# Turning six rows of modulation sums per layer in the down projection, behind units 8 to 13

## The chip, the cores and the metric

The kernel runs on one core of a Trainium2 chip. The metric is the device time of one execution in microseconds (us). The core has four computing engines that work side by side, each through its own instructions in order, and that wait for one another on semaphores: TensorE (PE in the profile; its weight loads are shown apart as PEld), VectorE (DVE), ScalarE (ACT) and GpSimd (POOL). SyncE (SP) issues the weight loads.

## What is computed

Two transformer blocks one after the other on 256 tokens of width 1024, all in float32. The first has two layers with a mixer and a feed-forward part each; the second is one layer whose norms are scaled and shifted by a modulation that hangs on a vector `c` alone:

```python
for l in range(DEPTH):                       # DEPTH = 2
    mixed = hybrid_mixer(x, mem, ...)
    x = layer_norm(ALPHA * x + mixed, ln1_g[l], ln1_b[l])
    ff = jnp.square(jax.nn.relu(x @ w_up[l])) @ w_down[l]      # 1024 -> 4096 -> 1024
    x = layer_norm(ALPHA * x + ff, ln2_g[l], ln2_b[l])
...
mod = (jax.nn.silu(c) @ ada_w + ada_b)[:, None, :]             # 1024 -> 6 * 1024, second block
```

## The kernel before

**Feed-forward units.** Each layer's feed-forward part runs in 16 units, u = 0 to 15 (`FFN_UNITS`): units 0 to 7 are the up projection, 8 to 15 the down projection (`UP_UNITS` = 8). A unit is one weight block of 1024 x 512. PE makes seven products of it instead of eight (`seven`, by sums and differences of quarter blocks); DVE makes the sums of the weight's quarters that this needs, four instructions in `weight_sums(u)` (L1335), one unit ahead: in its step u it calls `weight_sums(u + 1)`. For an up unit DVE then puts the seven products together (`combine`); for down units it does so in the last two steps only, since the others add up in the accumulators.

**Modulation.** The matrix `ada_w_2` is loaded beside, in twelve blocks of 1024 x 512, six per layer, j = 0 to 5, at the positions `ADA_POSITIONS` = 1, 3, 5, 8, 10, 12 among the units. ACT scales the eight slices of a block by silu(c) (`ada_scale`, L890). DVE adds the eight slices up to one row of 512 per partition (`ada_sums(j)`, L1277, three instructions, in step u = `ADA_POSITIONS[j]`) and writes it to one of two buffers, `ada_rows`, which lie in the tile `pre`. PE turns the row by four 128 x 128 transposes into the bank `ptb` (`ada_turned(j)`, L2630), and DVE reduces the bank to four columns of `mod` (`ada_columns(j)`, L1287). There is one such bank, so PE waits on `ada_back` before it turns row j until DVE has reduced row j - 1:

```python
pe.wait_ge(ada_summed, len(ADA_AT) * l + j + 1)
if l or j:
    pe.wait_ge(ada_back, len(ADA_AT) * l + j)
```

PE turns row j behind unit `ADA_POSITIONS[j]` + 1, that is behind units 2, 4, 6, 9, 11 and 13; DVE reduces it in step `ADA_POSITIONS[j]` + 2, that is 3, 5, 7, 10, 12 and 14.

**DVE's order in step u** (L1559): `ada_sums` if u is one of the positions, `weight_sums(u + 1)`, `ada_columns` if it is due, in layer 1 `bias_steps` in steps 9, 11 and 13, and `combine` where there is one.

**Weight loads.** All weights come through `ring`, three slots of 2 MB, in the order of use, modulation blocks among them; SP issues each load when its slot is free (`slot_free`, L459). The slot of a unit is freed by PE: the first product of the next unit carries the increment of `used` (`to_release` in `mm`, L2190; the transposes of a turning do not carry it). The slot of a modulation block is freed by DVE's last sum. In the down projection, the load for unit u + 2 goes into the slot of unit u, as in 8 and 10 or 10 and 12.

**POOL** makes the token-side sums of the down projection, one group of four for each pair of units; the later groups wait for the end of an odd unit.

Of the kernel before, what the change touches and what calls it, by code (L numbers as in the profile page):

```python
# [14 lines left out]
ALU = mybir.AluOpType  # L15
# [5 lines left out]
P = 128  # L21
# [14 lines left out]
UCOLS = 512  # L36
# [7 lines left out]
UP_UNITS, DOWN_UNITS = FF // UCOLS, 2 * (FF // (UROWS * P))  # L44
# [42 lines left out]
FFN_AT, ADA_AT = ffn_positions()  # L87
# [7 lines left out]
ADA_POSITIONS = [*ADA_UP, *(UP_UNITS + j for j in ADA_DOWN)]  # L95
# [104 lines left out]
def build(nc, a, out, stop=None):  # L200
    with ExitStack() as ctx:
# [8 lines left out]
        ident = sb("ident", [P, P])  # L210
# [9 lines left out]
        st = sb("st", [P, 2, T])  # L220
# [42 lines left out]
        kiz = sb("kiz", [P, 2, T])  # L263
        widx = sb("widx", [P, TT, 16])
        pre = sb("pre", [P, 2, 2, T + TAPS2 - 1])
# [27 lines left out]
        otok = hid[:, 16:24, :].rearrange("p a b -> p (a b)").rearrange("p (t d) -> p t d", t=TT)  # L293
        mod = sb("mod", [P, DEPTH, 24])
        silc = sb("silc", [P, 2, DC])
        ada_rows = pre[:, :, :, :].rearrange("p a b c -> p (a b c)")[:, 0:2 * UCOLS].rearrange("p (i n) -> p i n", i=2)
        nm = sb("nm", [P, 2, 2])
        zz = sb("zz", [P, 2, 2])
        rz = sb("rz", [P, 2, 2])
# [22 lines left out]
        ptb = ctx.enter_context(nc.psum_tensor("ptb", [P, 4, P], F32))  # L322
# [74 lines left out]
        ada_summed, ada_full, ada_back = sem("ada_summed"), sem("ada_full"), sem("ada_back")  # L397
# [830 lines left out]
        def _(dve):  # L1228
            steps = Steps(dve, dve_seq)
            tt, ts, stt = dve.tensor_tensor, dve.tensor_scalar, dve.scalar_tensor_tensor  # L1230
# [5 lines left out]
            for m in range(2):  # L1236
                dve.wait_ge(pe_begun, m + 1)
                j = 2 * m + 1
# [7 lines left out]
            for t in range(TT):  # L1246
                ins = dve.bn_aggr(mv[:, t, :], bn[:, t, :, :].rearrange("p a b -> p (a b)"))
# [29 lines left out]
            def ada_sums(j):  # L1277

                n = ADA_AT[j]
                dve.wait_ge(loaded[n % RING], 16 * (LAYER_UNITS // RING * l + n // RING + 1))  # L1280
                w = ring[:, n % RING]
                dve.wait_ge(ada_scaled, DC * (len(ADA_AT) * l + j + 1))
                for width in (4, 2):
                    steps.link(tt(w[:, 0:width, :], w[:, 0:width, :], w[:, width:2 * width, :], ALU.add))  # L1284
                tt(ada_rows[:, j % 2, :], w[:, 0, :], w[:, 1, :], ALU.add).then_inc(ada_summed, 1)

            def ada_columns(j):  # L1287

                dve.wait_ge(ada_full, len(ADA_AT) * l + j + 1)
                dve.tensor_reduce(mod[:, l, 4 * j:4 * j + 4], ptb[:, :, :], X, ALU.add).then_inc(ada_back, 1)  # L1290
# [177 lines left out]
            for l in range(DEPTH):  # L1468
# [90 lines left out]
                for u in range(FFN_UNITS):  # L1559
                    if u in ADA_POSITIONS:  # L1560
                        ada_sums(ADA_POSITIONS.index(u))
                    if u + 1 < FFN_UNITS:
                        weight_sums(u + 1)
                    if u - 2 in ADA_POSITIONS:
                        ada_columns(ADA_POSITIONS.index(u - 2))
                    if l == DEPTH - 1 and u in (9, 11, 13):
                        bias_steps((u - 9) // 2)
                    if u < UP_UNITS:
                        combine(u)
                    elif u >= FFN_UNITS - 2:  # L1570
                        h = u - (FFN_UNITS - 2)
                        if h == 0:
                            dve.wait_ge(xaff_ready, 4 * (l + 1))
                            combine(UP_UNITS, lambda: with_x(0, 0, pair01))
                        else:
                            def top_half():
                                with_x(0, 1, pair01)
                                token_mean2(0)
                            combine(UP_UNITS + 1, top_half)
                        dve.wait_ge(mz_free, GROUPS * l + UP_UNITS + h + 2)  # L1580
                        with_x(1, h, pair45)
                        if h == 0:
                            for t in range(TT):
                                dve.wait_ge(y_ready, 4 * l + 1 + t)
                                steps.mark(dve.bn_stats(bn[:, t, 0, :], ytok[:, t, 0, :]))
                            if l == DEPTH - 1:
                                bias_steps(3)
                                bias_steps(4)
# [261 lines left out]
            for u in range(2):  # L1850
                k, c = u - 2, 4 * u
# [257 lines left out]
            for t in range(TT):  # L2109
                for h in range(2):  # L2110
                    n = 2 * t + h
# [15 lines left out]
                for j in range(2, 4):  # L2127
                    dve.wait_ge(turn_full, 4 + (4 + 1 if t else j + 1))
                    for i in range(2):
                        c = 2 * j + i  # L2130
# [54 lines left out]
        def _(pe):  # L2185
# [43 lines left out]
            for j in range(4):  # L2229
                b = scr[j // 2] if j % 2 else head_bank()  # L2230
                for i in range(2):
                    for t in range(TT):
                        c = 2 * j + i
                        ins = pe.transpose(b[:, i, t * P:(t + 1) * P], mtok[:, t, c * P:(c + 1) * P], ident[:, :])
# [32 lines left out]
            b = head_bank()  # L2267
            for i in range(2):
                ins = pe.transpose(b[:, i, 0:127], prow[0:127, i, :], ident[0:127, 0:127])
            ins.then_inc(filled, 1)  # L2270
            for i, n in ((2, 123), (3, 128), (4, 33)):
                b = head_bank()
# [3 lines left out]
            for j in range(4):  # L2276
                b = head_bank()
                for i in range(2):
                    for t in range(TT):
                        c = 2 * j + i  # L2280
                        ins = pe.transpose(b[:, i, t * P:(t + 1) * P], xtok[:, t, c * P:(c + 1) * P], ident[:, :])
# [139 lines left out]
            for l in range(DEPTH):  # L2421
# [63 lines left out]
                else:  # L2485
                    w = next_unit()
# [4 lines left out]
                    b = free_bank()  # L2491
# [60 lines left out]
                for k in range(STEPS + 2):  # L2552
# [13 lines left out]
                    if k in (4, 6, 8, 10):  # L2566
                        h = (k - 4) // 2
                        b = free_bank()
# [10 lines left out]
                    elif k == 3:  # L2579
# [3 lines left out]
                        b = free_bank()  # L2583
                        for c in range(2):
                            ins = pe.matmul(b[:, 0, :], ones[:, 1, :], cy[:, c, :], start=c == 0, stop=c == 1)
# [7 lines left out]
                    elif k == 6:  # L2593
                        pe.wait_ge(csq_ready, l + 1)
                        b = free_bank()
                        for c in range(2):
                            ins = pe.matmul(b[:, 0, :], ones[:, 1, :], csq[:, c, :], start=c == 0, stop=c == 1)
# [32 lines left out]
                def ada_turned(j):  # L2630

                    pe.wait_ge(ada_summed, len(ADA_AT) * l + j + 1)
                    if l or j:
                        pe.wait_ge(ada_back, len(ADA_AT) * l + j)
                    for c in range(4):
                        ins = pe.transpose(ptb[:, c, :], ada_rows[:, j % 2, c * P:(c + 1) * P], ident[:, :])  # L2636
                    ins.then_inc(ada_full, 1)

                for u in range(FFN_UNITS):
                    assert units_done[0] == FFN_AT[u]  # L2640
                    w = next_unit()
                    t, t_base = tsum[u % 2], 4 * (FFN_UNITS * l + u)
                    if u < UP_UNITS:
                        for order in (("m1", "m2"), ("m4", "m5", "m7", "m6", "m3")) if u == 0 else (usual,):
                            seven(w, t, t_base, GROUPS * l + u, 1 - u % 2, pv_z[:, 0, :], True, True,
                                  x[:, 0:4, 0:H], x[:, 4:8, 0:H], x[:, 4:8, H:T], [sx[:, i] for i in range(4)],
                                  sx_ready, 4 * l, order, True, True,
                                  ((xlow_ready, DC * l), (xhigh_ready, DC * l)) if u == 0 else (None, None),
                                  a22_written=(xhigh_ready, DC * l + 4) if u == 0 else None)
                            if u == 0 and "m1" in order:  # L2650
                                features_back(1, 1)
                                features_back(1, 0)
                    else:
                        q, h = (u - UP_UNITS) // 2, (u - UP_UNITS) % 2
                        c, first, last = 8 * q, q == 0, q == 3
                        seven(w, t, t_base, GROUPS * l + UP_UNITS + h, 1 - h, pv_z[:, h, :], first and h == 0, last if h else first,
                              hid[:, c:c + 4, 0:H], hid[:, c + 4:c + 8, 0:H], hid[:, c + 4:c + 8, H:T],
                              [sh[:, q % 2, 0], sh[:, q % 2, 1], hid[:, c:c + 4, H:T], sh[:, q % 2, 2]],
                              sh_ready, 16 * l + 4 * q, usual, first, last, tokens=True)
                    to_release[0] += 1  # L2660
                    if u - 1 in ADA_POSITIONS:
                        ada_turned(ADA_POSITIONS.index(u - 1))
                    if u in ADA_POSITIONS:
                        assert units_done[0] == ADA_AT[ADA_POSITIONS.index(u)]
                        units_done[0] += 1
# [65 lines left out]
            for n, c in enumerate((4, 5, 0, 1)):  # L2731
                pe.wait_ge(xsq_sum, n // 2 + 1)
                ins = mm(ms, ones[:, 0, :], ysq[:, c, :], n == 0, n == 3)
# [4 lines left out]
            w = next_unit()  # L2738
            features(w, [0, 1], y, (h2_ready, 0))
            b = free_bank()  # L2740
            for k in range(DC):
                mm(b[:, 0, :], w[:, k, 256:384], y[:, k, :], k == 0, k == DC - 1)
            for k in range(DC):
                ins = mm(b[0:112, 1, :], w[:, k, 384:496], y[:, k, :], k == 0, k == DC - 1)
# [5 lines left out]
            b = mean_squares(None, 0, 1, latsq[0], 2, which=1, last=False)  # L2750
# [9 lines left out]
            b = free_bank()  # L2760
            for t in range(TT):
                pe.transpose(b[:, 0, t * P:(t + 1) * P], kvn[:, t * P:(t + 1) * P], ident[:, :])
            for t in range(TT):
                ins = mm(b[:, 1, 48 * t:48 * t + 48], kvki[64:112, 1, t * P:(t + 1) * P], ident[64:112, 64:112], True, True)
            ins.then_inc(filled, 1)
            b = free_bank()
# [371 lines left out]
```

## Time and profile before

| | us |
|---|---|
| median of 3 runs (lowest to highest) | 1309.13 (1308.36 to 1311.02) |
| the profiled execution | 1308.58 |
| its span | 1306.6 |
| PE busy in the span | 1293.0 |
| DVE busy | 941.5 |
| ACT busy | 426.4 |
| POOL busy | 185.2 |

The profile is one execution seen by the hardware's profiler. Its page gives busy times, the chain of work that ended last (followed back from the last instruction to what released it) and the costliest groups of instructions. The rows in order of time show for each engine the start, the length, the line of the kernel, what is written from what, and in brackets how long the engine idled before and what ended that. Rows of like instructions are merged, with their count. PE's matmuls overlap their weight loads, so the pauses of PE are best read from the starts of the weight loads (PEld).

### The profile page before, as it was taken

The page shows a single profiled execution, that of the slowest core. Times are in us where ns is not written, and L with a number is a line of the kernel's source. Part 1 is how long each engine was busy: PE and PEld are TensorE (multiplying, and loading weights), DVE is VectorE, ACT ScalarE, POOL GpSimd, SP SyncE. Part 2 cuts the span into 40 slices and gives each one's busy share as a digit, 9 for nine tenths or more (in the row PEclk, how much of TensorE's full clock was granted, in tenths as well). Part 3 has the DMA queues.
Part 4 walks back from the last instruction along what each step waited for, and adds up shares of the span by engine and source line. Part 5 has one row for each costly group of instructions (what it writes and reads, how often), then busy time and mean ns, then how long its engine had stood idle before and what let it go on. Part 6 is the DMA issues. An engine that isn't in the chain of part 4 may idle for free.

```text
span 1306.6 us, 32615 instructions
## 1 busy us (share of the span) xinstructions
PE 1293.0 (99%) x14429; PEld 1153.6 (88%) x14429; DVE 941.5 (72%) x1602; ACT 426.4 (33%) x929; POOL 185.2 (14%) x164
## 2 busy tenths in 40 slices
PE   8999999999999999999999999999999999999998
PEld 7975899988898589998877899999999986999986
DVE  3985798556688479857881799788888845866753
ACT  2254334220226433332055424455742103100101
POOL 3100422030000042204134000003200100011100
PEclk9999999999999999999999999999999999999999
DMA  9632567576433257767638895137645554645540
GB/s 326 202 130 97 194 239 278 206 267 238 163 129 129 97 195 260 260 223 268 216 98 241 220 248 150 60 121 253 208 134 186 175 192 130 194 151 176 179 178 32
DMA packets 132923, 243.06 MB, mean 186 GB/s; under 512 B 7237, under 2 KB 37725, under 8 KB 132273
## 3 DMA queue, kind: packets, MB, share of 16 engines
q1 hardware_dynamic: 122506, 218.00, 48.7%
q0 software_dynamic: 9872, 22.80, 7.4%
q8 instruction: 114, 1.87, 0.6%
q14 instruction: 24, 0.20, 0.1%
q10 hardware_dynamic: 407, 0.20, 0.1%
HBM read 231.49 MB, written 6.34 MB: 182 GB/s over the span
## 4 chain that ended last, share of the span: by engine, by line
PE 91%; DVE 5%; DMA 1%; ACT 1%; POOL 1%; issue 1%; SPq 0%; DVEq 0%
PE acc L2192 56%; PE scr L2192 17%; PE pvw L2192 9%; DVE mid L1512 2%; PE ptb L2306 1%; PE scr L2804 1%; PE pvw L2811 1%; DMA ring<-in_w_mem_kv 1%; PE scr L2297 1%; PE ptb L2192 1%; PE pvw L2316 1%; PE ptb L2636 0%; DMA strip_rows<-hid 0%; DVE hid L1860 0%; PE pvw L2322 0%
## 5 line engine op out<-in xcount | busy, mean ns | idle before, releaser
L2192 PE MATMUL acc<-y,ring 128*64 128x128 f32 (+3 forms) x1760 | 154.5, 285 | 0.0
L2192 PEld LDWEIGHTS acc<-y,ring 128*64 128x64 f32 (+2 forms) x1760 | 141.8, 152 | 7.7 <-ACT y L959 1.2
L2192 PE MATMUL acc<-ring,big 128*128 128x256 f32 (+1 forms) x376 | 115.6, 453 | 0.0
L2192 PEld LDWEIGHTS acc<-ring,big 128*128 128x128 f32 x376 | 70.6, 190 | 33.4 <-issue 27.0
L2192 PE MATMUL acc<-ring,hid 128*128 128x256 f32 (+1 forms) x364 | 99.1, 417 | 0.0
L2192 PE MATMUL acc<-x,ring 128*64 128x128 f32 (+1 forms) x1472 | 98.9, 278 | 0.0
L2192 PEld LDWEIGHTS acc<-x,ring 128*64 128x64 f32 (+1 forms) x1472 | 89.6, 139 | 4.7 <-issue 3.2
L895 ACT ACTIVATE ring<-ring,silc 128x512 f32<-128x512 f32 x96 | 60.1, 709 | 95.2 <-DMA ring<-in_ada_w 95.1
L2192 PEld LDWEIGHTS acc<-ring,hid 128*128 128x128 f32 x364 | 68.4, 190 | 22.2 <-issue 14.9
L2192 PE MATMUL acc<-ysq,ring 128*64 128x128 f32 x1248 | 75.0, 273 | 0.1
L2192 PEld LDWEIGHTS acc<-ysq,ring 128*64 128x64 f32 x1248 | 69.8, 137 | 0.4 <-ACT ysq L1076 0.4
L1284 DVE TENSOR_TENSOR ring<-ring 128x2048 f32<-128x2048 f32 (+1 forms) x24 | 44.1, 1836 | 33.5 <-ACT ring L895 32.9
L2192 PE MATMUL scr<-ysq,ring 128*64 128x128 f32 x1056 | 63.8, 273 | 0.0
L2192 PEld LDWEIGHTS scr<-ysq,ring 128*64 128x64 f32 x1056 | 59.3, 137 | 0.0
L1512 DVE SCALAR_TENSOR_TENSOR mid<-upad,pc,mid 128x256 f32<-128x256 f32 x120 | 48.7, 477 | 0.0
L1135 ACT ACTIVATE big<-acc 128x512 f32<-128x512 f32 x19 | 11.3, 596 | 109.7 <-PE acc L2192 109.7
L1344 DVE TENSOR_TENSOR ring<-ring 128x1024 f32<-128x1024 f32 x32 | 46.5, 1454 | 0.0
L1343 DVE TENSOR_TENSOR mid<-ring 128x1024 f32<-128x1024 f32 x16 | 19.5, 1222 | 37.1 <-DMA ring<-in_w_down 24.6
L720 ACT ACTIVATE work<-work,nm 128x256 f32<-128x256 f32 x80 | 39.6, 497 | 19.3 <-DVE nm L1258 15.6
L575 POOL TENSOR_TENSOR big<-hid 128x512 f32<-128x512 f32 x8 | 15.4, 1931 | 209.0 <-PE pvw L2192 147.9
L2192 PE MATMUL acc<-mid,ring 128*128 128x128 f32 (+2 forms) x384 | 42.4, 283 | 0.0
L2192 PEld LDWEIGHTS acc<-mid,ring 128*128 128x128 f32 (+1 forms) x384 | 39.6, 178 | 1.3
(581 smaller groups left out, 2767.5 us busy)
## 6 DMA issues: line engine op xcount, KB each, us to landing
ring<-in_w_in SPq DMA_DIRECT2D x24, 2048.0 KB, 11.4
ring<-in_w_up SPq DMA_DIRECT2D x16, 2048.0 KB, 8.5
ring<-in_w_down SPq DMA_DIRECT2D x16, 2048.0 KB, 8.0
ring<-in_ada_w SPq DMA_DIRECT2D x12, 2048.0 KB, 13.4
ring<-in_w_ffn_in SPq DMA_DIRECT2D x22, 1024.0 KB, 6.9
ring<-in_w_out SPq DMA_DIRECT2D x6, 2048.0 KB, 8.2
ring<-in_w_o_ssd SPq DMA_DIRECT2D x4, 2048.0 KB, 9.1
ring<-in_w_ffn_out SPq DMA_DIRECT2D x4, 2048.0 KB, 7.8
```

Of the source, the lines that this page charges most:

```text
L575: pool.tensor_tensor(s1, a21, a22, ALU.add).then_inc(sh_ready, 1)
L720: ins = act.activation(pr[:, i % 2, j, :], lg[:, i % 2, j, :], ACT.Exp, scale=-1.0, bias=nm[:, i % 2, j:j + 1], accum_out=zz[:, i % 2, j:j ...
L895: act.activation(ring[:, n % RING, k, :], ring[:, n % RING, k, :], ACT.Copy, scale=silc[:, 1, k:k + 1]).then_inc(ada_scaled, 1)
L1284: steps.link(tt(w[:, 0:width, :], w[:, 0:width, :], w[:, width:2 * width, :], ALU.add))
L1343: tt(t[:, 0], b12, b11, ALU.subtract).then_inc(t_ready, 1)
L1344: tt(b12, b22, b12, ALU.subtract).then_inc(t_ready, 1)
L1512: ins = stt(cy[:, c, :], upad[:, c, tap:tap + T], w, cy[:, c, :], ALU.mult, ALU.add)
L2192: ins = pe.matmul(dst, w, m, start=start, stop=stop, is_transpose=turned, skip_group_check=True)
L2297: ins = pe.matmul(scr[m][:, t, :], q[half, t * P:(t + 1) * P], keys[half, h, :], start=True, stop=True)
L2306: ins = pe.transpose(ptb[:, 2 * j + kt, :], at[:, i % 2, j, kt * P:(kt + 1) * P], ident[:, :])
L2316: ins = pe.matmul(pvb[:, 0, :], vt[:, h * P:(h + 1) * P], pt[:, i % 2, kt, :], start=kt == 0, stop=kt == TT - 1)
L2804: ins = pe.matmul(scr[i % 2][:, m, :], q2[:, 2 * j + m, t * P:(t + 1) * P], kvn[:, :], start=True, stop=True)
```

## The change

The rows go to four buffers instead of two; the two new ones lie in the tiles `kiz` and `st`. All six turnings of a layer stand behind down units: row j is turned behind unit 8 + j, units 8 to 13, and DVE reduces it in step 9 + j, steps 9 to 14, still behind `weight_sums`. The waits in `ada_turned` and in `ada_columns` stay as they are. The sums of the rows stay in their steps.

```diff
-        ada_rows = pre[:, :, :, :].rearrange("p a b c -> p (a b c)")[:, 0:2 * UCOLS].rearrange("p (i n) -> p i n", i=2)
+        pre_flat = pre[:, :, :, :].rearrange("p a b c -> p (a b c)")
+        ada_rows = [pre_flat[:, 0:UCOLS], pre_flat[:, UCOLS:2 * UCOLS], kiz[:, :, :].rearrange("p a t -> p (a t)"),
+                    st[:, :, :].rearrange("p a t -> p (a t)")]
...
-                tt(ada_rows[:, j % 2, :], w[:, 0, :], w[:, 1, :], ALU.add).then_inc(ada_summed, 1)
+                tt(ada_rows[j % 4], w[:, 0, :], w[:, 1, :], ALU.add).then_inc(ada_summed, 1)
...
                     if u + 1 < FFN_UNITS:
                         weight_sums(u + 1)
-                    if u - 2 in ADA_POSITIONS:
-                        ada_columns(ADA_POSITIONS.index(u - 2))
+                    if 0 <= u - 1 - UP_UNITS < len(ADA_AT):
+                        ada_columns(u - 1 - UP_UNITS)
...
                     for c in range(4):
-                        ins = pe.transpose(ptb[:, c, :], ada_rows[:, j % 2, c * P:(c + 1) * P], ident[:, :])
+                        ins = pe.transpose(ptb[:, c, :], ada_rows[j % 4][:, c * P:(c + 1) * P], ident[:, :])
                     ins.then_inc(ada_full, 1)
...
                     to_release[0] += 1
-                    if u - 1 in ADA_POSITIONS:
-                        ada_turned(ADA_POSITIONS.index(u - 1))
+                    if 0 <= u - UP_UNITS < len(ADA_AT):
+                        ada_turned(u - UP_UNITS)
```


## Rows read from the trace of the kernel before

**Rows 1.** the page: PE busy; the chain that ended last, by engine

```profile
PE 1293.0 (99%) x14429; PEld 1153.6 (88%) x14429; DVE 941.5 (72%) x1602; ACT 426.4 (33%) x929; POOL 185.2 (14%) x164
...
PE 91%; DVE 5%; DMA 1%; ACT 1%; POOL 1%; issue 1%; SPq 0%; DVEq 0%
```

**Rows 2.** PEld by time, layer 0, up projection: start, length, work, [gap before]

```profile
173.44 1.81 PEld L2192 LDWEIGHTS scr<-ysq,ring 128*64 128x64 f32 x32
...
175.19 1.81 PEld L2192 LDWEIGHTS pvw<-x,mid 128*64 128x64 f32 x32
...
177.17 0.42 PEld L2636 LDWEIGHTS ptb<-ident,pre 128*128 128x128 f32 x4 [0.17 <-issue]
...
177.75 1.73 PEld L2192 LDWEIGHTS acc<-x,ring 128*64 128x64 f32 x32 [0.17 <-issue]
```

**Rows 3.** the same view, down projection of layer 0, starts of units and turnings

```profile
252.49 1.70 PEld L2192 LDWEIGHTS acc<-ring,hid 128*128 128x128 f32 x8
...
262.85 1.70 PEld L2192 LDWEIGHTS pvw<-work,hid 128*128 128x128 f32 x8
...
264.58 0.57 PEld L2636 LDWEIGHTS ptb<-ident,pre 128*128 128x128 f32 x4
...
265.12 1.60 PEld L2192 LDWEIGHTS acc<-ring,hid 128*128 128x128 f32 x8
...
277.10 1.70 PEld L2192 LDWEIGHTS acc<-ring,hid 128*128 128x128 f32 x8
...
301.72 1.70 PEld L2192 LDWEIGHTS acc<-ring,hid 128*128 128x128 f32 x8
...
314.35 1.60 PEld L2192 LDWEIGHTS acc<-ring,hid 128*128 128x128 f32 x8
```

**Rows 4.** DVE in order of time, down projection of layer 0, same columns

```profile
261.31 1.23 DVE L1343 TENSOR_TENSOR mid<-ring 128x1024 f32<-128x1024 f32 x1 [4.05 <-DMA ring<-in_w_down]
...
271.78 3.55 DVE L1284 TENSOR_TENSOR ring<-ring 128x2048 f32<-128x2048 f32 x2 [5.71 <-ACT ring L895]
...
275.98 1.22 DVE L1343 TENSOR_TENSOR work<-ring 128x1024 f32<-128x1024 f32 x1
...
280.64 0.68 DVE L1290 TENSOR_REDUCE mod<-ptb 128x4 f32<-128x512 f32 x1
...
310.65 1.23 DVE L1343 TENSOR_TENSOR mid<-ring 128x1024 f32<-128x1024 f32 x1 [4.79 <-DMA ring<-in_w_down]
```

**Rows 5.** SP's queue in order of time: two merged issues of weight loads

```profile
265.86 12.45 SPq L475 DMA_DIRECT2D ring<-in_w_down  x2
```

**Rows 6.** us to landing: issued at 265.86, at 254, all of 240 to 330

```profile
ring<-in_w_down SPq DMA_DIRECT2D x1, 2048.0 KB, 7.8
...
ring<-in_ada_w SPq DMA_DIRECT2D x1, 2048.0 KB, 12.9
...
DMA to landing us min/median/max: 7.8/8.0/13.0
```

**Rows 7.** DVE in order of time, down projection of layer 1

```profile
596.80 4.50 DVE L1284 TENSOR_TENSOR ring<-ring 128x2048 f32<-128x2048 f32 x2 [2.44 <-ACT ring L895]
...
606.61 0.68 DVE L1290 TENSOR_REDUCE mod<-ptb 128x4 f32<-128x512 f32 x1
```

**Rows 8.** POOL in order of time, down projection of layer 1

```profile
596.80 3.42 POOL L580 TENSOR_TENSOR big<-hid,big 128x512 f32<-128x512 f32 x1
```

**Rows 9.** PE's weight loads in order of time, layer 1: units 9 and 11

```profile
577.43 1.70 PEld L2192 LDWEIGHTS acc<-ring,hid 128*128 128x128 f32 x8
...
602.04 1.70 PEld L2192 LDWEIGHTS acc<-ring,hid 128*128 128x128 f32 x8
```

**Rows 10.** busy time by stretch: engines' us (instructions), granted clock, DMA share, GB/s

```profile
0.00:1300.00 1300.00, 1292.75 (x14429) 1153.64 (x14429) 937.56 (x1595) 424.99 (x923) 185.21 (x164) 1.00 0.57 186
...
1300.00:1306.60 6.60, 0.23 (x2) 0.00 (x0) 3.93 (x8) 1.43 (x6) 0.00 (x0) 0.70 0.43 159
```

**Rows 11.** PE's waits: for whom, total us, times, longest

```profile
PE pvw L2226 <- DVE upad L1234: 1.8, 1, 1.8
```


## The prediction

> **What bounds the kernel now.** The page comes first: PE is busy in 99% of the span, and the chain of work that ended last lies 91% on PE [rows 1]. So a change counts if it makes PE's row of products shorter or opens a hole in it. Next I read PE's weight loads in order of time, because they show where PE pauses. In the up projection one product follows the other every 1.75 us (173.44 to 175.19), but where a turning of a modulation row stands between two units the pitch is 2.56 (175.19 to 177.75) [rows 2]: the turning costs 0.81, of which two gaps of 0.17 stand before and behind its four transposes. In the down projection the pitch is 1.727 ((262.85 - 252.49) / 6), and with a turning 2.27 (262.85 to 265.12): 0.54, without such gaps [rows 3]. The up projection works in tiles 64 columns wide and the transposes in tiles of 128, as the down projection does; that is the one visible difference. Last I read what DVE does in the down projection, because the change makes PE wait for a DVE instruction there [rows 4].
>
> **The change part by part.**
>
> **1. Twelve turnings, all behind down units.** Six (three in each of two layers) move from a place of 0.81 to one of 0.54: 6 x 0.27 = 1.6 us saved, if nothing else moves. The transposes and their loads are the same 4 each. No DMA is issued in them.
>
> **2. Three reductions per layer leave the up projection on DVE** (0.68 us each). PE covers them: its products follow one another there with no other gap than those at the turnings [rows 2], so I take cost and gain as nothing. Had PE been late for DVE there, it would be a gain of at most 6 x 0.68 = 4 us; that is the lower bound. PE arrives 0.81 earlier after each turning removed; the weight loads are released by PE and shift with it, so DVE shifts too. Two more buffers: the sums are written as before, at the same length.
>
> **3. The wait.** This decides. Turning j on PE waits for `ada_back` of j - 1, because both use the one bank `ptb`: PE may not overwrite it until DVE has reduced row j - 1 into `mod`. Before, a unit or more lay between a turning and the next, and the reduction was long done. Now turning j stands behind unit 8 + j, the reduction of j - 1 in DVE's step u = 8 + j, **behind** `weight_sums(9 + j)` and, for j = 2 and 4, behind `ada_sums` too. DVE works in order, so PE, which has no need yet of these weight sums, now waits for them at the end of the unit. What is queued behind PE's wait is everything: the next unit's products, and its first product frees the ring slot of the unit just done, so the next weight load on SP's queue waits too. POOL's and ACT's work is released by the same events, relative to the unit, as before.
>
> How late is DVE? I count from the start S of PE's first product in the unit.
>
> *Odd turnings (1, 3, 5).* Unit 9 starts at 252.49 and PE gets to its end at 264.58, 12.09 later [rows 3]. The first product of unit 9 frees the slot for the load of unit 10: issue comes 0.74 after the start (265.12 [rows 3] to 265.86 [rows 5]) and landing 7.8 after the issue [rows 6]. So DVE starts `weight_sums(10)` at 261.31, 8.82 after S, after 4.05 us of idling for that load [rows 4]. The four sums take 4.66 up to the next instruction (275.98 to 280.64 [rows 4]). The reduction that now stands behind them would start at 13.48 and end, 0.68 later, at 14.16. PE is there at 12.09. It waits 2.1, plus the semaphore's way, which I set at 0.1 (bounds 0 and 0.2, the order of the 0.17 gaps in [rows 2]).
>
> *Even turnings (2, 4).* Here DVE has first to sum the modulation weights, whose load is issued behind that of unit 10 and takes 12.9 to land [rows 6]; ACT scales them, and DVE idles for ACT until 271.78 [rows 4]. None of this hangs on when unit 10 starts, only on S of unit 9. The reduction that follows today starts at 280.64, 28.15 after 252.49 [rows 3, 4]. In the new order one stands at the same place: end 28.15 + 0.68 = 28.83, with the semaphore 28.93, and the turning of 0.54 makes unit 11 start at **29.47** after unit 9's start. Before: 277.10 - 252.49 = **24.61** [rows 3]. So a pair of units gets **4.86 us** longer. The odd wait inside the pair isn't added: what PE loses at turning 1 it would else lose at turning 2. Only the load for unit 11 could follow it: it is issued when unit 10 starts, 14.80 + 0.74, lands 7.8 later at 23.34, and DVE wants it at 23.49 (275.98 - 252.49). It fits, by 0.15; a load half a us longer would add 0.35 per pair.
>
> *Layer 1.* The same chain, a little longer: the first two sums of the modulation weights take 4.50 there [rows 7] instead of 3.55 [rows 4], beside a POOL sum of 3.42 that starts with them [rows 8], and the reduction starts at 606.61 [rows 7], 29.18 after unit 9's start at 577.43 [rows 9]. 29.18 + 0.68 + 0.1 + 0.54 = 30.50 against 602.04 - 577.43 = 24.61 [rows 9]: **5.89 us** per pair. POOL's work is released by the end of unit 9, so I leave the collision in.
>
> *The last, turning 5,* stands behind unit 13 and waits for the reduction in step 13: unit 13 starts at 301.72, DVE gets its load at 310.65, 8.93 later [rows 3, 4]; + 4.66 + 0.68 + 0.1 + 0.54 = 14.91 to the start of unit 14, against 314.35 - 301.72 = 12.63 [rows 3]: **2.28 us**. Layer 1 shows the same pattern, so twice.
>
> **The sum.** Two pairs per layer: 2 x 4.86 + 2 x 5.89 = 21.5. Two last ones: 4.6. These hold the turnings 1 to 5 on both sides. Outside them: six turnings of 0.81 gone from the up projection (-4.9), turning 0 behind unit 8 new (2 x 0.54 = +1.1). Net 21.5 + 4.6 - 4.9 + 1.1 = **+22.3 us**. The profiled execution took 1308.58 (span 1306.6), 0.04% below the median of 1309.13, so I use it as it is: 1308.6 + 22.3 = **1330.9 us**. Bounds of this case: without the collision on POOL in layer 1 2 x 1.03 less, a DVE gain in the up projection 4 less; slower loads in four pairs 1.4 more, semaphore 0.2 instead of 0.1 another 0.6, and 2 for what the stages behind make of it: some 1325 to 1335.
>
> **The rivals.**
>
> *No wait, only the gain.* If each reduction were done when PE comes, 1308.6 - 1.6 = **1307.0**. It decides at 12.09 us after the unit's start: load and weight sums and reduction together would have to fit, which now take 8.82 + 4.66 + 0.68 = 14.16; the load would have to land in 5.6 instead of 7.8. Against it speaks that no load of this stretch landed in less than 7.8 [rows 6]. For it, only that I could have misread which step the reduction stands in. 5%.
>
> *The clock falls in the holes.* The granted clock is 1.00 from 0 to 1300 us, and 0.70 in the last 6.6 us, where PE does two instructions [rows 10]: so the lower level (1.2 GHz) exists and comes when PE stops. The longest wait of PE in the trace is 1.8 us [rows 11]; the new ones are 2 to 3. The Trainium skill ("TensorE: Matmul & The Clock Gate", section on HAM oscillation) tells of a matmul loop that waits for a load in each step and starts every step at the lower clock; by that rule this change would pay at each hole once more. The price from rows: a product of 1.73 at half the clock takes 1.73 more; one such behind each of ten waits makes +17, **1348**. Nothing in this trace shows a fall in a hole inside the work, and PE was busy for twelve us before each. 7%.
>
> *The change does less than it says:* part of the waits is met, since sums or loads run faster when PE leaves more time between units, some 10 us in all: **1319**. The load rows speak against it. 5%.
>
> **How the numbers follow.** My forecast holds 83%, the three rivals 5, 7 and 5%. About 0.2% (2.6 us) is what a measurement here can tell from no change: the first rival lies within it, all else is slower. Faster 2%, same 5%, slower 93%. The range starts from 1325 to 1335, with some 4 at either end for what the bounds don't know: 1321 to 1339. That leaves out the first two rivals, part of the third, and a few per cent of the forecast: some 18%.
>
> **What would show it.** Right: idle time of PE before the turning's line, put down to DVE's write of `mod`, ten times (turnings 1 to 5 in two layers) with some 2 us at each; unit 9 to unit 11 some 29.5 us apart in layer 0 and 30.5 in layer 1; up units with no turning between them and no gap; the granted clock at 1.00 throughout. Wrong: units in the down projection still 12.1 us apart with turnings between them (then the reduction isn't behind the weight sums), or products longer than 1.73 behind the holes (then the clock).

## The result and the profile after

The changed kernel takes 1332.63 us (median of 4 runs, 1330.51 to 1335.57) against 1309.16 before: a ratio of 1.018, 95% interval 1.0168 to 1.0192. It is 23.5 us slower. The profiled execution took 1333.1, its span is 1331.1, 24.5 more than the span before.

Four lines of the page after, to be read beside [rows 1]: PE's busy time and share, the granted clock in 40 slices, and the chain that ended last, by engine and by line. A slice is 33 us long, so a fall of the clock for a few us does not show in that row.

```profile
PE 1298.3 (98%) x14429; PEld 1156.5 (87%) x14429; DVE 938.6 (71%) x1602; ACT 426.2 (32%) x929; POOL 181.2 (14%) x164
...
PEclk9999999999999999999999999999999999999999
...
PE 78%; DVE 10%; DMA 7%; ACT 2%; issue 2%; POOL 1%; SPq 0%; DVEq 0%
PE acc L2194 49%; PE scr L2194 14%; PE pvw L2194 7%; DMA ring<-in_ada_w 4%; DVE mid L1514 2%; ACT ring L897 1%; DVE ring L1286 1%; DMA ring<-in_w_down 1%; PE ptb L2308 1%; PE pvw L2813 1%; PE scr L2806 1%; DMA ring<-in_w_mem_kv 1%; DVE ring L1346 1%; PE scr L2299 1%; PE ptb L2194 1%
```

PE does the same 14429 instructions, and its share of the chain falls from 91 to 78%. What has come in is DVE, ACT and a load: `ring<-in_ada_w`, the load of the modulation block, now has 4% of the span. Work that ran beside PE has got onto the path. The list of PE's waits (for whom: us in total, times, longest) says at which point:

```profile
PE ptb L2638 <- DVE mod L1292: 18.6, 10, 3.2
```

Ten waits of the turning for DVE's write of `mod`, as many as there are turnings 1 to 5 in two layers. Such a row does not exist in the kernel before, whose longest wait is the one in [rows 11]. In order of time, PE's weight loads in the down projection of layer 0 (start, length, work, gap before), to be read beside [rows 3]:

```profile
250.50 0.57 PEld L2638 LDWEIGHTS ptb<-ident,pre 128*128 128x128 f32 x4
251.04 1.60 PEld L2194 LDWEIGHTS acc<-ring,hid 128*128 128x128 f32 x8
...
265.24 0.42 PEld L2638 LDWEIGHTS ptb<-ident,pre 128*128 128x128 f32 x4 [2.25 <-issue]
265.63 1.60 PEld L2194 LDWEIGHTS acc<-ring,hid 128*128 128x128 f32 x8
...
279.92 0.42 PEld L2638 LDWEIGHTS ptb<-ident,kiz 128*128 128x128 f32 x4 [2.33 <-issue]
280.31 1.60 PEld L2194 LDWEIGHTS acc<-ring,hid 128*128 128x128 f32 x8
...
294.75 0.42 PEld L2638 LDWEIGHTS ptb<-ident,st 128*128 128x128 f32 x4 [2.48 <-issue]
295.13 2.48 PEld L2194 LDWEIGHTS acc<-ring,hid 128*128 128x128 f32 x8
297.70 2.44 PEld L2194 LDWEIGHTS acc<-ring,big 128*128 128x128 f32 x8
300.17 1.70 PEld L2194 LDWEIGHTS acc<-ring,hid 128*128 128x128 f32 x8
...
309.40 0.42 PEld L2638 LDWEIGHTS ptb<-ident,pre 128*128 128x128 f32 x4 [0.63 <-issue]
309.79 1.60 PEld L2194 LDWEIGHTS acc<-ring,hid 128*128 128x128 f32 x8
...
324.38 1.60 PEld L2194 LDWEIGHTS acc<-ring,hid 128*128 128x128 f32 x8
```

In these rows a line with `ptb<-ident` is a turning, and the one behind it is the first product of the next unit. Turning 0 (250.50) has no gap. Turning 1 stands behind a gap of 2.25, turning 2 behind 2.33. Unit 9 starts at 251.04, unit 11 at 280.31, 29.27 later; before it was 24.61. DVE in the same stretch, to be read beside [rows 4]:

```profile
259.77 1.23 DVE L1345 TENSOR_TENSOR mid<-ring 128x1024 f32<-128x1024 f32 x1 [4.51 <-DMA ring<-in_w_down]
...
264.44 0.68 DVE L1292 TENSOR_REDUCE mod<-ptb 128x4 f32<-128x512 f32 x1
...
279.12 0.68 DVE L1292 TENSOR_REDUCE mod<-ptb 128x4 f32<-128x512 f32 x1
```

The reduction at 264.44 stands at the end of the four weight sums that waited 4.51 us for a load, and PE turns the next row 0.8 us after that start (265.24). The chain that ended last, in order of time, runs through the other one, at 279.12: from the load of the modulation block over ACT's scaling and DVE's sums (start, us, what):

```profile
252.19 12.94 DMA ring<-in_ada_w
...
265.15 5.02 ACT ring L897 x8
...
270.26 2.30 DVE ring L1286
...
279.12 0.69 DVE mod L1292
```

In the up projection, the pitch from the last product of a unit to the first of the next is 1.74 now, where it was 2.56 [rows 2]:

```profile
199.86 1.81 PEld L2194 LDWEIGHTS pvw<-x,mid 128*64 128x64 f32 x32
201.60 1.81 PEld L2194 LDWEIGHTS acc<-x,ring 128*64 128x64 f32 x32
```

### The profile page after: what moved, and what is told of

It is laid out like the page before. It is cut to its first block, busy times and chain, and to the rows that moved or that the text cites. A ratio compares the mean times of both kernels' runs of the same rounds, so it can differ in the third digit from the quotient of the medians.

```text
span 1331.1 us, 32615 instructions
## 1 busy us (share of the span) xinstructions
PE 1298.3 (98%) x14429; PEld 1156.5 (87%) x14429; DVE 938.6 (71%) x1602; ACT 426.2 (32%) x929; POOL 181.2 (14%) x164
## 4 chain that ended last, share of the span: by engine, by line
PE 78%; DVE 10%; DMA 7%; ACT 2%; issue 2%; POOL 1%; SPq 0%; DVEq 0%
PE acc L2194 49%; PE scr L2194 14%; PE pvw L2194 7%; DMA ring<-in_ada_w 4%; DVE mid L1514 2%; ACT ring L897 1%; DVE ring L1286 1%; DMA ring<-in_w_down 1%; PE ptb L2308 1%; PE pvw L2813 1%; PE scr L2806 1%; DMA ring<-in_w_mem_kv 1%; DVE ring L1346 1%; PE scr L2299 1%; PE ptb L2194 1%
## 5 line engine op out<-in xcount | busy, mean ns | idle before, releaser
L2194 PE MATMUL acc<-ring,hid 128*128 128x256 f32 (+1 forms) x364 | 102.5, 429 | 0.0
L881 ACT ACTIVATE pt<-acc 128x512 f32<-128x512 f32 x20 | 11.7, 586 | 97.0 <-PE acc L2194 97.0
```

Of the source, the lines that this page charges most:

```text
L2194: ins = pe.matmul(dst, w, m, start=start, stop=stop, is_transpose=turned, skip_group_check=True)
```

## The experiments

**Where the reduction stands in DVE's order.** The changed kernel, with DVE's step in another order:

```diff
+                    if 0 <= u - 1 - UP_UNITS < len(ADA_AT):
+                        ada_columns(u - 1 - UP_UNITS)
                     if u in ADA_POSITIONS:
                         ada_sums(ADA_POSITIONS.index(u))
                     if u + 1 < FFN_UNITS:
                         weight_sums(u + 1)
-                    if 0 <= u - 1 - UP_UNITS < len(ADA_AT):
-                        ada_columns(u - 1 - UP_UNITS)
```

> The changed kernel (1332.6 us) with one thing moved: in each step DVE reduces the row that is due before it makes the sums of the modulation block and of the next weight, not behind them. Turnings, buffers and waits are those of the changed kernel. Theory (the reduction's place in DVE's order makes PE wait): no wait of PE on the write of mod is left, and the six turnings that moved out of the up projection are won: 1309.2 - 1.7 = 1307.5. Rival (six turnings in a row, or slots freed behind turnings, slow the down projection): it stays within some us of 1332. Rival (the clock that falls in holes is most of the loss): 1307.5 too, so it is told apart by the next two runs and not by this one.

Measured: 1307.26 us (11 runs, 1306.26 to 1307.54) against 1309.10, ratio 0.9984 (0.9975 to 0.9993). PE's weight loads at turnings 1 and 2 of layer 0:

```profile
262.58 0.57 PEld L2638 LDWEIGHTS ptb<-ident,pre 128*128 128x128 f32 x4
...
275.11 0.57 PEld L2638 LDWEIGHTS ptb<-ident,kiz 128*128 128x128 f32 x4
```

The six turnings of a layer follow one another behind down units, 12.53 apart, with no gap before any, in layer 1 too. So neither the number of turnings there nor the slots freed behind them cost anything beyond the length of the turnings themselves; the order of one DVE instruction did. This kernel is the fastest of the study, 1.8 us faster than before.

**The buffers alone.** The kernel before with four buffers for the rows, turned and reduced at the old places (the hunks on `ada_turned` and `ada_columns` undone).

> The kernel before with the change's four buffers alone; turnings and reductions at their old places. Theory and rivals agree: same as before, 1309.2 within 0.5 us. If it is slower, part of the loss lies in where the rows are kept.

Measured: 1309.24 against 1309.10, ratio 1.0002 (0.9993 to 1.0011). Where the rows are kept costs nothing that shows, to about 0.1%.

**Do the ten waits add up?** Two kernels with a part of the reductions ahead. `due` is the row to be reduced:

```diff
+                    due = u - 1 - UP_UNITS
+                    if 0 <= due < len(ADA_AT) and due % 2 == 0:
+                        ada_columns(due)
                     if u in ADA_POSITIONS:
                         ada_sums(ADA_POSITIONS.index(u))
                     if u + 1 < FFN_UNITS:
                         weight_sums(u + 1)
-                    if 0 <= u - 1 - UP_UNITS < len(ADA_AT):
-                        ada_columns(u - 1 - UP_UNITS)
+                    if 0 <= due < len(ADA_AT) and not (due % 2 == 0):
+                        ada_columns(due)
```

> The changed kernel with only the reductions of rows 0, 2 and 4 moved ahead of the sums; those of rows 1 and 3 stay behind them. So the waits before turnings 1, 3 and 5 are gone and those before turnings 2 and 4 stay. Theory (a pair of units is as long as the chain of load, scaling, sums and reduction counted from its start; the first wait of a pair adds nothing): pairs stay at 29.3 to 31.4 us, the waits at turnings 2 and 4 grow from 2 to 3 us to some 4 to 5, and only the last waits of a layer are won, 14.59 + 15.21 - 2 x 12.63 = 4.5: 1328, up to 1331 if the clock falls in the longer holes. Rival (ten waits that add up, 18.6 us in all in the profile): six of them with some 2 us each go, 1320.

Measured: 1330.48 (1328.56 to 1331.77), ratio 1.0163 (1.0149 to 1.0177). Six of the ten waits are gone and only 2.2 us with them. PE's list of waits has four now, and PE's weight loads in layer 0 show the two of that layer grown:

```profile
PE ptb L2641 <- DVE mod L1292: 16.6, 4, 4.9
```

```profile
250.68 1.60 PEld L2197 LDWEIGHTS acc<-ring,hid 128*128 128x128 f32 x8
...
262.66 0.57 PEld L2641 LDWEIGHTS ptb<-ident,pre 128*128 128x128 f32 x4
...
279.44 0.42 PEld L2641 LDWEIGHTS ptb<-ident,kiz 128*128 128x128 f32 x4 [4.28 <-issue]
279.83 1.60 PEld L2197 LDWEIGHTS acc<-ring,hid 128*128 128x128 f32 x8
...
308.55 0.71 PEld L2641 LDWEIGHTS ptb<-ident,pre 128*128 128x128 f32 x4 [4.23 <-issue]
309.24 2.78 PEld L2197 LDWEIGHTS acc<-ring,hid 128*128 128x128 f32 x8
312.05 1.70 PEld L2197 LDWEIGHTS acc<-ring,big 128*128 128x128 f32 x8
```

Turning 1 (262.66) does not wait. Turning 2 waits 4.28 where it waited 2.33, and the pair from unit 9 (250.68) to unit 11 (279.83) stays as long: 29.15, where the changed kernel has 29.27. The other three pairs are 29.41, 30.12 and 31.13, beside 29.48, 30.54 and 31.37 there. The first wait of a pair adds nothing, as the theory says; 1320 is refuted. The last rows belong to the clock, below.

The mirror image has `due % 2 == 1` in both places.

> The mirror image: only the reductions of rows 1 and 3 ahead of the sums; rows 0, 2 and 4 behind. Waits stay before turnings 1, 3 and 5 and go before 2 and 4. Theory: a pair is now 14.6 + 12.6 = 27.2 us instead of 29.3 to 31.4 in the changed kernel, the last one stays: 1332.6 - (29.27 + 29.48 + 30.54 + 31.37 - 4 x 27.2) = 1320.7; holes of about 2.2 only, so the granted clock stays at 1.00. If waits added up one by one, four waits of 2 to 3 us go: some 1322 as well; this run is there for the size of the pair and for the clock in short holes.

Measured: 1324.29 (4 runs: 1318.82, 1328.21, 1325.03, 1323.56), ratio 1.0127 (1.0111 to 1.0142). The profiled execution is the one of 1318.82, and its clock is 1.00 throughout. Its turnings 1, 2 and 3 in PE's weight loads:

```profile
265.24 0.42 PEld L2641 LDWEIGHTS ptb<-ident,pre 128*128 128x128 f32 x4 [2.28 <-issue]
...
277.61 0.58 PEld L2641 LDWEIGHTS ptb<-ident,kiz 128*128 128x128 f32 x4
...
292.33 0.42 PEld L2641 LDWEIGHTS ptb<-ident,st 128*128 128x128 f32 x4 [2.22 <-issue]
```

Gaps of 2.28 and 2.22 at turnings 1 and 3, none at turning 2; turnings 1 and 3 are 27.09 apart, and the theory wanted 27.2 for a pair. The size holds, but the median is 3.6 above what I expected, and the executions lie 9 us apart, where those of the kernel before differ by 2.7. The mean granted clock of each execution is on record: 0.999, 0.998, 0.996 and 0.995, from the shortest to the longest. So the 1.00 that I expected held in the profiled execution, and not in all.

**The clock in the holes.** In the changed kernel's profile four products last longer than 1.73, behind three holes: 295.13 and 297.70 above take 2.57 and 2.47 to the next, and in layer 1 those at 617.29 and 648.66 (rows further down) take 2.99 and 2.67. The stretches behind two of these holes (busy us of PE, PEld, DVE, ACT, POOL; granted clock, DMA share, GB/s), beside one that has no hole:

```profile
236.00:250.00 14.00, 14.00 (x101) 12.49 (x98) 5.48 (x7) 7.10 (x11) 0.00 (x0) 1.00 0.42 151
294.70:300.20 5.50, 5.42 (x20) 4.57 (x21) 0.46 (x1) 4.94 (x8) 4.22 (x4) 0.69 0.57 178
647.90:651.40 3.50, 3.41 (x12) 3.00 (x13) 0.00 (x0) 0.00 (x0) 0.00 (x0) 0.59 0.15 13
```

The granted clock is below 1.00 in the last two: PE had stood for 2.5 and 3.5 us, and then ran for a while at the lower of its two levels, 1.2 instead of 2.4 GHz. The kernel that waits 4.2 at turning 4 shows it too (308.55: the product behind it takes 2.81). To see what it costs, I filled the holes: matmuls on zeros (a constant tile `zeros`) are added to a sum that is open, ahead of each wait. In the changed kernel, for turnings 1 to 5 (in the kernel with rows 1 and 3 ahead, the condition is `if j % 2:`):

```diff
                 def ada_turned(j):
 
+                    if j:
+                        for _ in range(8):
+                            pe.matmul(acc[2][:, 0, :], zeros[:, :], x[:, 0, :], start=False, stop=False, skip_group_check=True)
                     pe.wait_ge(ada_summed, len(ADA_AT) * l + j + 1)
```

I first took eight, since I put the product of 1.73 down as eight matmuls; the rows count two weight loads for each, so it is four.

> The kernel with only the reductions of rows 1 and 3 ahead, whose executions took 1318.8 to 1328.2, with eight matmuls on a tile of zeros (8 x 0.22 = 1.7 us, added to an open sum, so nothing changes in it) ahead of each of its six waits of 2.2: PE works through most of the wait. Theory (the holes themselves cost what the profile of 1318.8 shows, at a granted clock of 1.00; the other executions lost 5 to 9 us because the clock fell behind holes): 1319 in all executions, granted clock 1.00. Rival (the spread has another cause, loads or DVE): 1319 to 1328 as before.

> The changed kernel (1332.6) with the same eight matmuls ahead of each of its ten waits. Theory (the next reduction is a fixed time behind a unit's start, so what the low clock costs is mostly hidden in the next wait): 1330 to 1331.5, granted clock 1.00. Rival (three stretches at the low clock cost their full 1.7 each): 1327.5.

Measured: 1328.27 (1327.59 to 1329.31) and 1343.07 (1342.69 to 1348.07), ratios 1.0149 (1.0135 to 1.0162) and 1.027 (1.0254 to 1.0285): slower. The filled hole in layer 0:

```profile
262.83 3.43 PEld L2638 LDWEIGHTS acc<-x,zeros 128*128 128x128 f32 x16
266.28 0.57 PEld L2643 LDWEIGHTS ptb<-ident,pre 128*128 128x128 f32 x4
```

Eight matmuls take 3.45, more than the hole, so they took the wait's place and tell nothing of the clock's price. They check the sum instead: with no wait left, six or ten times 3.45 over the kernel with the reductions ahead is 1307.3 + 20.7 = 1328.0 and 1307.3 + 34.5 = 1341.8, so 0.3 and 1.3 under what was measured. The execution of 1348.07 has a granted clock of 0.998, the same as that of 1342.69: a long execution need not be the clock's. With four (`range(4)`) they fit:

> The kernel with only rows 1 and 3 reduced ahead, with four matmuls on zeros (they take 0.43 us each, the traces of the two kernels with eight show; so 1.7 us) ahead of each of its six waits of 2.2. Theory (the clock falls behind some of the holes, and not always): with shorter holes 1319 in all executions, granted clock 1.00. Rival (the spread of 1318.8 to 1328.2 has another cause): it stays.

> The changed kernel (1332.6) with four matmuls on zeros, 1.7 us, ahead of each of its ten waits. Theory (the wait is set by a chain counted from a unit's start; three stretches at the low clock are mostly hidden in the next wait, beside some 0.5 us of later slot release each): 1330 to 1331.5, granted clock 1.00, waits of some 0.5 left. Rival (each such stretch costs its full 1.7): 1327.5 or less.

Measured: 1319.41 (1318.72 to 1320.30), ratio 1.008 (1.0065 to 1.0095), for the kernel with half the waits; and 1329.57 (1329.08 to 1329.89), ratio 1.0157 (1.014 to 1.0174), for the changed kernel. In the two profiled executions the granted clock is 1.00 from the start to 1310 and 1322 us. So the spread of the first is gone, and its size of 1319 came as expected. The changed kernel has won 3.1 us: more than the 1.1 to 2.6 that I expected, less than the 5.1 of the rival. In its list of waits there is this left, four short ones behind the zeros in place of ten:

```profile
PE ptb L2643 <- DVE mod L1294: 3.1, 4, 1.3
```

Its unfilled twin again:

> The kernel with only rows 1 and 3 reduced ahead once more, unchanged. Theory: executions between 1319 and 1328 again; a profiled one shows stretches at the low clock of 3.4 us behind holes, and is longer than 1318.8 by some 1.5 us for each of them, since no wait follows a turning 2 or 4 that could hide them. Rival (loads or DVE): longer without such stretches.

> One more look at the kernel with only rows 1 and 3 reduced ahead, whose profiled executions so far (1318.8 and 1320.2) were those with no stretch at the low clock, while others took up to 1328.2. Theory: if this one is above 1322, its profile shows such stretches behind holes, 1.2 to 1.7 us longer for each; if it is below, none. Rival: longer without them.

Measured: 1321.43 (1319.44 to 1326.53), ratio 1.0101 (1.0079 to 1.0124), and 1319.80. The spread came again. But the profiled executions, 1320.23 and 1319.80, are again among the shortest, and neither shows the low clock. No execution of this kernel above 1321 has a profile, so no row shows a fall in it. The mean granted clocks do: over all its runs they are 0.999 in the four executions of 1318.8 to 1320.2, 0.998 at 1322.6 and 1323.6, 0.996 at 1325.0 and 1326.5, and 0.995 at 1328.2, where the four of the filled twin have 0.998 or 0.999. So the three longest did run in part at the low clock. That this is all of their extra time is not shown: 0.004 of some 1320 us is 5 us (an estimate from these numbers), and the longest is 9 us longer than the shortest.

**What a turning costs in either projection.** The kernel with the reductions ahead, and twelve turnings of a constant more, ahead of the fifth product of a unit; what they write is not used:

```diff
+                def more_turnings(count):
+                    if count:
+                        pe.wait_ge(ada_back, count)
+                    for c in range(4):
+                        pe.transpose(ptb[:, c, :], ident[:, :], ident[:, :])
...
                     elif m == "m5":
+                        if before_m5 is not None:
+                            before_m5()
```

> The kernel with the reductions ahead (1307.3 us) with twelve more turnings of a constant tile into the free bank, one inside each of the up units 1 to 6 of both layers, ahead of the fifth of the seven products. What they write is not used. It prices a turning among products of 64 columns: by the starts of weight loads in the kernel before, 0.73 to 0.81 each (three made the up projection 2.2 longer), so +8.8 to +9.7: 1316.1 to 1317.0. Rival (a turning costs the same everywhere, four transposes of 0.14): 12 x 0.55 = +6.6, 1313.9.

> The same with the twelve more turnings inside the down units 9 to 14, ahead of the fifth product, where products are 128 columns wide. By the pitch in the kernel before, 0.44 to 0.54 each: +5.3 to +6.5, 1312.6 to 1313.8, some 3 us below its twin in the up projection. Rival (same cost everywhere): no difference between the two.

Measured: 1315.49 against 1308.88, ratio 1.005 (1.0037 to 1.0064), in the up projection; 1311.65, ratio 1.0021 (1.0013 to 1.003), in the down projection. Against the kernel before they differ by +6.6 and +2.8, their base by -1.8: (6.6 + 1.8) / 12 = 0.70 us for a turning in the up projection, (2.8 + 1.8) / 12 = 0.38 in the down projection. The two in PE's weight loads, first up, then down:

```profile
172.41 0.42 PEld L2648 LDWEIGHTS ptb<-ident 128*128 128x128 f32 x4 [0.17 <-issue]
173.00 1.73 PEld L2194 LDWEIGHTS scr<-ysq,mid 128*64 128x64 f32 x32 [0.17 <-issue]
174.69 1.78 PEld L2194 LDWEIGHTS scr<-ysq,ring 128*64 128x64 f32 x32
```

```profile
256.92 0.57 PEld L2647 LDWEIGHTS ptb<-ident 128*128 128x128 f32 x4
257.47 1.60 PEld L2194 LDWEIGHTS scr<-work,big 128*128 128x128 f32 x8
259.09 1.70 PEld L2194 LDWEIGHTS scr<-ring,hid 128*128 128x128 f32 x8
```

Two gaps of 0.17 among products of 64 columns, none among those of 128. The prices are 0.11 and 0.16 under what I read from the pitch (0.81 and 0.54). The product behind a turning comes 0.06 and 0.11 shorter (1.69 instead of 1.75, 1.62 instead of 1.73); the other 0.05 is open.

## Why the prediction was right

The forecast was 1330.9 in a range of 1321 to 1339; measured 1332.6. Its mechanism, the reduction behind the weight sums, is shown by the move of that one instruction (1332.6 to 1307.3). Term by term, from the starts of units in PE's weight loads; after, layer 1, where the turning at 647.96 stands behind the longest of the ten holes:

```profile
586.75 1.60 PEld L2194 LDWEIGHTS acc<-ring,hid 128*128 128x128 f32 x8
...
601.37 1.60 PEld L2194 LDWEIGHTS acc<-ring,hid 128*128 128x128 f32 x8
...
617.29 2.96 PEld L2194 LDWEIGHTS acc<-ring,hid 128*128 128x128 f32 x8
...
647.96 0.72 PEld L2638 LDWEIGHTS ptb<-ident,pre 128*128 128x128 f32 x4 [3.53 <-issue]
648.66 2.64 PEld L2194 LDWEIGHTS acc<-ring,hid 128*128 128x128 f32 x8
...
663.87 1.60 PEld L2194 LDWEIGHTS acc<-ring,hid 128*128 128x128 f32 x8
```

| term | forecast | profile after | holes filled |
|---|---|---|---|
| pair of units, layer 0 | 29.47, twice | 29.27, 29.48 | 29.16, 29.10 |
| pair of units, layer 1 | 30.50, twice | 30.54, 31.37 | 30.33, 30.15 |
| last (unit 13 to 14), layers 0 and 1 | 14.91, twice | 14.59, 15.21 | 14.53, 14.54 |

The last column is the changed kernel with four matmuls on zeros.

*The chains* were sized to 0.4 us each, a little too long: with no low clock (last column) every term lies 0.2 to 0.4 under the forecast, 2.0 in all. The turning behind a hole takes 0.39 up to the next product (265.24 to 265.63), not the 0.54 that I took from a place without a hole.

*That the first wait of a pair is not added* was a choice worth some 9 us: four such waits of 2.2 would have come on top. The run with only rows 0, 2 and 4 ahead shows that it was right.

*The saving in the up projection* was 4.9 in the forecast. The layer 0 of the profile shows 2.2 (from 154.23 to 240.51 before and 154.44 to 238.52 after), so 4.4 for both; in layer 1 PE lost 0.5 of it again in one wait of that execution, for a DVE sum:

```profile
505.95 1.73 PEld L2194 LDWEIGHTS acc<-ysq,mid 128*64 128x64 f32 x32 [0.53 <-DVE mid L1348]
```

The price per turning was read 0.11 and 0.16 too high, as the two runs with more turnings say; its difference between the projections, 0.27 in the forecast, is 0.32.

*The clock* is the term that I got wrong, though the range held it. I made it a rival with a chance of 7%, as something that happens behind every hole and costs 17 us, or not at all, and left it out of the sum; that PE is busy for twelve us ahead of each hole, which I held against it, did not prevent it. Of my signs, the ten waits and the lengths of the pairs came, but the clock of 1.00 throughout did not, and the products longer than 1.73 came, which I had put down as a sign against the forecast. It happened behind three of the ten holes in the profiled execution, and cost the changed kernel 3.1 us (1332.6 with holes, 1329.6 with filled ones). That is by medians: its four executions have mean granted clocks from 0.998 (1330.51, the shortest) to 0.993 (1335.57, the longest). Products and transposes in these three stretches took 1.7, 1.7 and 1.4 us longer, 4.7 in all, so the price of one, 1.73 in the rival, was about right; by the table, units 9 to 14 of the two layers got 73.34 + 77.12 - 72.79 - 75.02 = 2.7 longer. The difference was hidden in the main: the next reduction comes at a time counted from a unit's start, so a unit that runs slower meets a shorter wait (0.63 at 309.40, where 2.3 would stand). What was not hidden came in part through SP: the slot is freed by the unit's first product, and at the low clock that is later. In layer 1 (two issues merged; the first at the row's start, the second 0.4 ahead of its end):

```profile
602.11 16.86 SPq L477 DMA_DIRECT2D ring<-in_w_down  x2
```

The load behind unit 9 is issued at 602.11, 0.74 after unit 10 starts (601.37); the one behind unit 10 near 618.6, 1.3 after unit 11 starts (617.29). That pair is the one of 31.37. Its modulation block also took 14.1 us to land, where the same block took 12.9 before; why is open. Against that, the collision with POOL that the forecast had in both pairs of layer 1 came in the first alone: DVE's first two sums take 4.50 there (605.98) and 3.55 in this pair (638.30); with the holes filled they take 4.66 in both.

So the mechanism and the size of the chains were right, and that +22.3 met +23.5 so closely is in part luck: chains 2.0 us too long, a saving 0.5 too large, and a clock cost of 3 that stood outside the sum nearly cancel. The Trainium skill ("TensorE: Matmul & The Clock Gate", section on HAM oscillation) describes a loop that waits for a load in each step and starts each step at the low clock. The trace agrees in part: three of ten holes were followed by the low clock, and behind the one at 294.75 the next wait was shorter by the 1.7 us that the products had lost (0.63 at 309.40).

*The rivals.* "No wait, only the gain" at 1307.0 is the kernel that reduces first, at 1307.26: its price was right, and in the changed kernel its condition was not met. "The change does less than it says" fell: the loads of `w_down` landed in 7.8 to 8.3 us after and in 7.8 to 8.4 before, apart from the last of each layer, which is issued 0.4 us behind another and took 13 to 14 in both kernels.

## What to carry to other kernels

When a step is moved, look past its cost at the waits that it brings along: follow the engine that must answer, and see what stands in its queue ahead of the answer, down to the load that this is waiting for. A one-line reduction behind work prepared for a later unit makes the later unit's load part of this unit's path. And price a repeated wait by the chain that sets it, not by its length: of two waits that were set from one common start only the last counted here.

## What the runs showed of the hardware

- Four 128 x 128 transposes among f32 products of 64 columns cost PE 0.70 us, among products of 128 columns 0.38.
- The low clock came behind holes of 2.5, 3.3 and 3.5 us in PE's work (of ten, 0.6 to 3.5 long, in the profile after) and behind three of four holes of 4.2 to 5.2 (rows 0, 2 and 4 ahead). It came behind none of the six holes of 2.0 to 2.5 in each of three profiled executions with rows 1 and 3 ahead, and behind none of the sixteen of 0.2 to 1.7 that were left beside the zeros. The same program had it in one execution and not in another: with rows 1 and 3 ahead the mean granted clock was 0.999 at 1318.8 us and 0.995 at 1328.2; behind which hole it fell there is not on record.
- With eight matmuls on zeros (3.45 us) in place of each of the ten holes the granted clock stayed at 1.00 throughout the work, where it fell behind the holes of 3.3 and 3.5 us.
